# A decoder trunk on one core: second tile's last 1024 columns scaled behind the first x tile's split, their eight transposes between the products of the first gate group

## The reference

```
for l in range(DEPTH):                                   # DEPTH = 2
    y = mixer_sublayer(x, w_in[l], ...)                  # 256 x 2048
    x = layer_norm(ALPHA * x + y, ln1_g[l], ln1_b[l])    # <- the norm of this change
    y = conv_ffn(x, w_gate[l], w_up[l], conv_w[l], conv_b[l], w_down[l])
    x = layer_norm(ALPHA * x + y, ln2_g[l], ln2_b[l])
```

## Time and profile before

| | us |
|---|---|
| median of 3 runs | 2208.43 (2207.94 to 2208.83) |
| profiled execution, its own time from first to last instruction (span) | 2207.2 |
| PE busy in it | 2190.5 (99%) |
| DVE busy | 1585.8 (72%) |
| ACT busy | 1078.5 (49%) |
| POOL busy | 244.7 (11%) |

### The profile page before, as it was taken

The page is one execution under the profiler, slowest core; times in us unless marked ns, Lnnn a source line. Parts: engine busy times, 40 slices in busy tenths (PEclk is TensorE's granted clock), DMA queues, the critical chain, the costliest instruction groups (busy, mean ns, idle before and its releaser), DMA issues.

```text
span 2207.2 us, 28550 instructions
## 1 busy us (share of the span) xinstructions
PE 2190.5 (99%) x11340; PEld 1876.2 (85%) x11340; DVE 1585.8 (72%) x2020; ACT 1078.5 (49%) x1353; POOL 244.7 (11%) x250
## 2 busy tenths in 40 slices
PE   9999999999999999999999999999999999999998
PEld 7888888888888888888888888888888888888886
DVE  6656688776666766887785566797866676668877
ACT  5444555544444444544464455554444444445444
POOL 1751010120000000000008410101200000000001
PEclk9999999999999999999999999999999999999999
DMA  8655564666666666666665555756666666666664
GB/s 272 202 163 162 154 238 153 182 190 191 191 191 191 191 191 210 201 200 200 211 195 166 168 159 149 246 153 190 188 189 188 190 190 190 191 210 204 197 208 173
DMA packets 207654, 420.95 MB, mean 191 GB/s; under 512 B 13056, under 2 KB 15136, under 8 KB 206496
## 3 DMA queue, kind: packets, MB, share of 16 engines
q1 hardware_dynamic: 204656, 406.37, 59.6%
q0 software_dynamic: 2432, 12.22, 1.5%
q10 hardware_dynamic: 432, 0.52, 0.1%
HBM read 416.97 MB, written 2.10 MB: 190 GB/s over the span
## 4 chain that ended last, share of the span: by engine, by line
PE 97%; DVE 2%; DMA 0%; ACT 0%; issue 0%; POOLq 0%; POOL 0%; DVEq 0%
PE ps L1665 29%; PE ps L1669 15%; PE ps L1551 14%; PE ps L1553 14%; PE ps L1552 14%; PE ps L1732 2%; PE ps L1734 2%; PE ps L1733 2%; PE ps L1596 1%; PE ps L1839 1%; PE ps L1813 1%; PE ps L1790 1%; PE ps L1710 0%; PE ps L1712 0%; PE ps L1711 0%; DMA raw<-in_w_out_dram 0%
## 5 line engine op out<-in xcount | busy, mean ns | idle before, releaser
L1010 DVE TENSOR_TENSOR wlo<-raw,whi 128x1024 fp32r<-128x1024 f32 x711 | 898.2, 1276 | 443.3 <-ACT whi L720 439.3
L720 ACT ACTIVATE whi<-raw 128x1024 fp32r<-128x1024 f32 x711 | 740.9, 1057 | 625.0 <-DMA raw<-in_w_up_dram 225.0
L1665 PE MATMUL ps<-xT,whi 128*128 128x512 f32 x2816 | 657.3, 390 | 0.0
L1665 PEld LDWEIGHTS ps<-xT,whi 128*128 128x128 f32 x2816 | 522.4, 188 | 104.5 <-ACT qkT L741 0.4
L1669 PEld LDWEIGHTS ps<-xT,wlo 128*128 128x128 f32 x2816 | 350.5, 192 | 7.5
L1669 PE MATMUL ps<-xT,wlo 128*128 128x256 f32 x2816 | 352.8, 283 | 0.0
L1551 PE MATMUL ps<-whi,xT 128*128 128x512 f32 x872 | 350.1, 401 | 0.0
L1553 PE MATMUL ps<-whi,xT 128*128 128x512 f32 x872 | 340.4, 390 | 0.0
L1552 PE MATMUL ps<-wlo,xT 128*128 128x512 f32 x872 | 339.6, 389 | 0.0
L1553 PE MATMUL ps<-whi,hT 128*128 128x512 f32 x520 | 202.3, 389 | 0.0
L1551 PE MATMUL ps<-whi,hT 128*128 128x512 f32 x520 | 202.3, 389 | 0.0
(11 more groups left out here) (273 smaller groups left out, 1810.6 us busy)
## 6 DMA issues: line engine op xcount, KB each, us to landing
raw<-in_w_gate_dram SPq DMA_DIRECT2D x176, 512.0 KB, 4.0
raw<-in_w_up_dram SPq DMA_DIRECT2D x176, 512.0 KB, 4.0
raw<-in_w_in_dram SPq DMA_DIRECT2D x175, 512.0 KB, 3.7
raw<-in_w_down_dram SPq DMA_DIRECT2D x132, 512.0 KB, 3.7
raw<-in_w_out_dram SPq DMA_DIRECT2D x52, 512.0 KB, 3.7
sraw<-in_w_down_dram SPq DMA_DIRECT2D x44, 512.0 KB, 5.6
oraw<-in_w_out_dram SPq DMA_DIRECT2D x12, 512.0 KB, 5.1
xres<-in_x_dram POOLq DMA_DIRECT2D x4, 512.0 KB, 6.5
```

Source lines behind the costliest of these rows:

```text
L720: act.activation(whi[:, s, :, :], raw[:, s, :, :], ACT.Copy).then_inc(hi_done, 1)
L1010: dve.tensor_tensor(wlo[:, s, :, :], raw[:, s, :, :], whi[:, s, :, :].bitcast(F32), ALU.subtract)\
L1665: return pe.matmul(ps[:, bank, :], whi[:, s, kk, m * P:(m + 1) * P], xT[:, kt, :, :].rearrange("p a s -> p (a s)"), start=kt == 0, stop=kt ...
```

## The change

DVE now scales tile 1's last 1024 columns after the split of the first x tile, in the mixer's norm only; in the norm behind the feed-forward part (`which == 1`) the order stays. PE turns only banks 0 to 3 of tile 1 ahead of the first gate group; the eight transposes of banks 4 to 7 go into the group, four ahead of the products of gate block 2 and four ahead of those of block 3. The number of instructions is the same. The code moves down by up to nine lines (line 1539 becomes 1547, 1665 becomes 1674, 1669 becomes 1678, 1311 becomes 1317).

```diff
-                    for c0, c1 in (((0, 2 * CW),), ((0, CW // 2), (CW // 2, 2 * CW), (2 * CW, D_MODEL)))[t]:
-                        dve.tensor_scalar(xres[:, t, c0:c1], xres[:, t, c0:c1], mv[:, t, 0:1],
-                                          lns[:, 2, t:t + 1], ALU.subtract, ALU.mult).then_inc(ln_done, 1)
+                    for c0, c1 in (((0, 2 * CW),), ((0, CW // 2), (CW // 2, 2 * CW)))[t]:
+                        normalise(t, c0, c1)
+                    if t == 1 and which == 1:
+                        normalise(1, 2 * CW, D_MODEL)
+
+            def normalise(t, c0, c1):
+
+                dve.tensor_scalar(xres[:, t, c0:c1], xres[:, t, c0:c1], mv[:, t, 0:1],
+                                  lns[:, 2, t:t + 1], ALU.subtract, ALU.mult).then_inc(ln_done, 1)
...
                 for j in range(GC):
                     if first:
                         x_split(layer, 1, j)
+                    if first and j == 0:
+                        normalise(1, 2 * CW, D_MODEL)
...
                 for m in (2, 3):
+                    turn_x(layer, 1, [(2 * m, 1), (2 * m + 1, 1)])
                     wait_read(pe, layer, m, ("xturn", 1))
...
                 turn_x(layer, 1, [(b, 0) for b in range(8) if b not in late] + [(b, 0) for b in late] +
-                       [(b, 1) for b in range(8)])
+                       [(b, 1) for b in range(4)])
```

## The result

The changed kernel takes 2211.61 us (median of 21 runs, 2209.18 to 2213.31) against 2208.21 us (21 runs, 2207.80 to 2209.19): ratio 1.0014, 95% interval 1.0008 to 1.0020. That is 3.4 us more, within 0.2%, where 1.8 us more was forecast. The runs also scatter more: 4.1 us from lowest to highest in place of 1.4.

A forecast was written before the change was run, and what follows sets the result against it. The prediction took PE, busy 99% of the span, to bound the kernel. Removal 0, DVE's earlier split 0 and eight transposes at 0.89 us per layer gave 2208.43 + 1.77 = 2210.2 us, range 2207.8 to 2212.4.

The forecast's parts named there:

- Removing the eight gives back 0: Ahead of the first gate product: without eight transposes the second product still waits for ACT until 379.22, gain 0.
- DVE's half gives 0: Ahead of the first x tile's split: moving 0.72 us of scaling gains 0, since the split waits for ACT's first copy.
- The eight cost 0.89 us per layer among the products: Between gate blocks 1, 2 and 3: eight transposes at 0.111 us each add 0.89 us per layer, 1.77 for both.
- the recorded length of 0.272 us: Other bound for one transpose between gate products: 0.272 us, paid in full if nothing overlapped; 0.111 was taken instead.
- No wait for the moved scaling or the later splits: In the first gate group: PE doesn't wait for DVE's later work, with slacks of some 0.4 and 0.56 us.
- rivals 1 and 2: Moved transposes hide in PE's waits for ACT (2209.3 or 2208.4 us, chance 0.12); DVE becomes late (2211.6 us, 0.06).
- The sum: Whole kernel: 0 removed, 0.89 us per layer added, DVE's earlier split 0; 2208.43 + 1.77 = 2210.2 us, chance 0.74.
- rival 2: First gate group: PE waits for DVE's later splits or scaling, at most 0.72 us per layer; 2211.6 us, chance 0.06.
- a wider spacing of the transposes: Between gate products: transposes at a spacing of 0.16 us, used with DVE's lateness for the range's upper end of 2212.4.
- there they cost nothing: In their old place ahead of the first gate product the eight are free, because PE waits for ACT until 379.22 anyway.
- The base of the sum: Whole kernel: the median of 2208.43 us, taken as 1.23 us above the profiled span of 2207.2 us.
- The range: Whole kernel: 2207.8 us (transposes fully hidden, less 0.5 scatter) to 2212.4 us (DVE late and transposes at 0.16 us spacing).

The follow-up runs named there:

- e3_skip8: The kernel before without the eight transposes of tile 1's banks 4 to 7, left out for good; 2209.60 us, ratio 1.0004.
- e2_pe_half: The changed kernel with DVE scaling the last 1024 columns ahead of the first split again, only PE's half left; 2211.57 us, ratio 1.0014.
- e9: The kernel before with only DVE's scaling moved behind the split, plus eight extra transposes between tile 1's banks 3 and 4; 2212.56 us, ratio 1.0018.
- e10: The kernel before with only DVE's scaling moved behind the split, plus eight extra transposes between tile 0's and tile 1's; 2213.88 us, ratio 1.0024.
- e1_fill: The changed kernel plus eight transposes that nobody reads, ahead of the first gate product where the moved eight stood; 2210.63 us, ratio 1.0008.
- e7_dve_half: The kernel before with only DVE's scaling moved behind the split, all 16 transposes of tile 1 ahead of the products; 2214.12 us, ratio 1.0026.

## Why the prediction was right or wrong

- *Removing the eight gives back 0:* right. The second product kept its 2.52 us, released by ACT's bank 1, and e3_skip8 without the eight has a stretch of 4.97 us.
- *DVE's half gives 0:* right. The hole of 0.60 us stood where 0.6 to 0.7 was expected, and e2_pe_half takes about as long as the whole change (3.02 against 3.40 us more), with the same 5.84 us in layer 0.
- *The eight cost 0.89 us per layer among the products:* right, 0.84 to 0.89 us in the stretches without a fall, and 5.84 us in layer 0 is the length that the prediction named. By the recorded length of 0.272 us it would have been 2.2 us; the spacing was the price.
- *No wait for the moved scaling or the later splits:* right. The scaling ended 0.5 us ahead of its readers, and rivals 1 and 2 did not come.
- *The sum:* the time was 3.40 us more where 1.77 was forecast, in the range and within 0.2%, as said. That it fell inside the range is luck in part: the upper end, 2212.4, was made of rival 2 and a wider spacing of the transposes, and neither came; that rival 2's price of 2211.6 is also the measured time is chance. The term that failed is one that the sum holds at nothing: a fall of the granted clock in PE's longer pause. What spoke against it was a wait before the change, 1.00 us long with the clock at 1.00 behind it. But that wait has transposes behind it and then products at once. The new pause, 0.52 to 0.56 us between matmuls and 0.73 to 0.77 between weight loads, stands right ahead of the products, after a seam in which PE had been idle for 1.00 us and its weight loads for another 0.39 already. The eight had cost no time there and still had a use: with them PE worked up to the first product. (That the place is what differs is shown by e9 and e10 for the long pause; for the short one e1_fill, 9 of 11 executions at 0.999, and e2_pe_half, 3 of 10, show that filling it helps.) The wait of 1.00 us is not what brings the fall: it is the longest in the changed kernel's seam, and the profile of e1_fill has it too, with the last pause filled, and no fall. The same term is the step "there they cost nothing", which asked only what the chain loses.
- *Its size:* where two stretches differ by a fall alone the runs give 1.28 to 1.61 us (7.31 - 5.84 and 7.32 - 5.84; 6.34 - 4.97; 7.15 and 7.11 - 5.83; 8.45 - 6.84; 8.39 - 6.83). 1.77 plus one such fall is 3.1 to 3.4 us, the figure of the first runs. Two further sets of runs gave 2.02 and 2.35: the share of executions with a fall differs from set to set (at 0.999 stand 4 of 21, 7 of 11 and 7 of 11), and the median moves with it. What decides between none, one and two is open.
- *The base of the sum:* the forecast took 1.23 us around the span. Every execution on record lies 1.97 to 2.16 us above its own span, so the profiled one of before took about 2209.2 us (an estimate: 2207.2 + 2.0), 1.0 us above the median of 2208.21. The sum stood on the median and was not touched by it.
- *The range:* its lower end by its own sum is 2208.4 - 0.5 = 2207.9, not 2207.8. Nothing hangs on it.

## What to carry to other kernels

Here work that hid in a wait of the busiest engine was free there (a stretch of 4.95 us with the eight transposes, 4.97 without) and cost its start-to-start time between products (0.105 to 0.111 us each); look at what releases the instruction behind it before moving it out. Instructions of PE ahead of a burst of products can have a second use: with a pause of 0.52 to 0.56 us in their place the granted clock fell from 1.00 to 0.50 at the start of the burst, in part of the executions; on a 2208 us kernel eight transposes decided over 1.3 to 1.6 us per seam. And where a change makes the scatter of the runs grow as well as the median, look at the granted clock of short stretches, and sort the executions by their mean clock: here one step in the third digit, 0.999 to 0.998, went with 1.6 us (1.75 to 3.31 more).

## What the runs showed of the hardware

- The granted clock fell to 0.50 behind a pause of 0.52 to 0.56 us between PE's matmuls before products (changed kernel, e2_pe_half, e3_skip8) or of 1.86 to 1.87 us before transposes (e7_dve_half, e10_half_early), at one, both or none of two like places in executions of one program, and returned to 1.00 within the stretch. It cost 1.28 to 1.61 us each time.
- Transposes whose results nobody reads kept the clock at 1.00 when they stood in the pause (e1_fill and e9_half_late: no fall in the profile, 9 of 11 executions at 0.999 each), and did not when they stood ahead of the long one (e10_half_early: a fall in the profile, 1 of 11 at 0.999).
- A float32 128x128 transpose between products costs 0.105 to 0.111 us of PE's time, though 0.272 us is recorded for it.
